# Pairing the head sums of queries and keys, and starting the last attention inside the projection before it

## The reference

```python
qkv_a, g_a, q_b, zf_fwd, zf_bwd, i_b, g_b, zgate_a, zgate_b = jnp.split(z, split_points, axis=-1)
qkv_a = qkv_a.reshape(B, S, N_GROUPS_2, 3, HEADS_PER_GROUP, HEAD_DIM)   # 3 groups, 8 heads, 64
for g, (window, dilation) in enumerate(ATTN_GROUPS):
    q = rms_norm(qkv_a[:, :, g, 0], q_norm_w[layer, g])
    k = rms_norm(qkv_a[:, :, g, 1], k_norm_w[layer, g])
    v = qkv_a[:, :, g, 2]
    o_g, m_g, d_g = dilated_window_attention(q, k, v, bias_tab[...], window, dilation)
...
o_a = jnp.sum(wts[..., None] * jnp.stack(outs), axis=0) / jnp.sum(wts, axis=0)[..., None]
y_a = (o_a * silu(g_a)) @ w_proj_a
...
y_b = (rms_norm(o_fwd + o_bwd, hg_norm_w) * silu(g_b)) @ w_proj_b
merged = sigmoid(zgate_a) * y_a + sigmoid(zgate_b) * y_b
h_res = h_res + merged @ w_out
```

## Time and profile before

| | us |
|---|---|
| median of 3 runs (lowest, highest) | 1845.63 (1845.46, 1846.04) |
| the profiled execution | 1845.46 |
| its span | 1843.7 |
| PE, PEld busy | 1722.3 (93%), 1435.8 (78%) |
| DVE, ACT busy | 1149.3 (62%), 1003.3 (54%) |
| POOL busy | 71.6 (4%) |
| mean granted clock of TensorE | 0.969 of full speed |

### The profile page before, as it was taken

How to read it: one execution, slowest core, us unless ns; L and a number is a source line. 1 busy time by engine, 2 the same in 40 slices (tenths; PEclk the granted TensorE clock), 3 DMA queues, 4 the chain that set the end, 5 groups by cost and what they waited for, 6 DMA issues and landing times.

```text
span 1843.7 us, 27871 instructions
## 1 busy us (share of the span) xinstructions
PE 1722.3 (93%) x11207; PEld 1435.8 (78%) x11212; DVE 1149.3 (62%) x1527; ACT 1003.3 (54%) x1314; POOL 71.6 (4%) x68
## 2 busy tenths in 40 slices
PE   6999989899999979999999699999979989999898
PEld 3786665698888748889869488888849978887588
DVE  5341664798989665333345698989855784534554
ACT  4323653488888644224343488888834562443452
POOL 0000000100000010000000000000010000100100
PEclk9999999899999979999999799999989999999999
DMA  8546004899999863223454499999944433353511
GB/s 332 193 122 228 1 15 196 326 400 406 408 404 407 333 282 120 101 100 137 182 215 186 160 364 408 406 407 405 378 171 180 180 144 139 86 212 137 146 61 69
DMA packets 53125, 421.76 MB, mean 229 GB/s; under 512 B 17044, under 2 KB 18196, under 8 KB 30624
## 3 DMA queue, kind: packets, MB, share of 16 engines
q1 hardware_dynamic: 26416, 364.55, 50.3%
q0 software_dynamic: 8592, 32.69, 5.6%
q10 hardware_dynamic: 18016, 23.07, 3.6%
HBM read 399.27 MB, written 21.02 MB: 228 GB/s over the span
## 4 chain that ended last, share of the span: by engine, by line
PE 82%; DVE 8%; ACT 4%; DMA 4%; issue 2%; POOL 1%; SPq 0%; ACTq 0%; DVEq 0%; POOLq 0%
PE ps L732 47%; PE ps L867 18%; PE ps L689 3%; DMA ring<-w_all 2%; PE ps L712 2%; PE ps L878 1%; PE ps L739 1%; DMA arena<-y_d,tok_row 1%; PE ps L723 1%; PE ps L1301 1%; PE ps L885 1%; PE ps L1103 1%; PE ps L1374 1%; PE ps L1132 1%; PE ps L1107 1%
## 5 line engine op out<-in xcount | busy, mean ns | idle before, releaser
L2211 DVE TENSOR_TENSOR w_lo<-ring,w_hi 128x1024 fp32r<-128x1024 f32 x384 | 452.5, 1219 | 55.4 <-ACT w_hi L1592 53.3
L1592 ACT ACTIVATE w_hi<-ring 128x1024 fp32r<-128x1024 f32 x384 | 396.3, 1057 | 97.3 <-PE ps L867 55.9
L732 PE MATMUL ps<-XT_lo,arena_r 128*128 128x256 f32 (+1 forms) x1712 | 386.5, 300 | 10.1 <-DVE ring_r L2081 7.2
L732 PEld LDWEIGHTS ps<-XT_lo,arena_r 128*128 128x128 f32 x1712 | 283.9, 190 | 25.9 <-issue 7.9
L867 PE MATMUL ps<-w_hi,x_hi 128*128 128x256 f32 (+1 forms) x768 | 248.5, 324 | 2.7 <-issue 2.6
L867 PE MATMUL ps<-w_lo,x_hi 128*128 128x256 f32 (+1 forms) x768 | 244.7, 319 | 0.0
L867 PE MATMUL ps<-w_hi,x_lo 128*128 128x256 f32 (+1 forms) x768 | 244.6, 319 | 0.0
L732 PE MATMUL ps<-arena_r 128*128 128x512 f32 (+1 forms) x656 | 233.1, 363 | 10.8 <-DVE XT_lo L2377 4.0
L2081 DVE TENSOR_TENSOR ring_r<-ring,arena_r 128x1024 fp32r<-128x1024 f32 x96 | 113.6, 1221 | 120.9 <-ACT arena_r L1494 120.8
L732 PE MATMUL ps<-XT_lo,ring_r 128*128 128x256 f32 x640 | 182.1, 285 | 0.0
L867 PEld LDWEIGHTS ps<-w_hi,x_hi 128*128 128x128 f32 x768 | 145.9, 190 | 19.4 <-DVE w_lo L2211 4.3
(11 more groups left out here) (350 smaller groups left out, 2690.3 us busy)
## 6 DMA issues: line engine op xcount, KB each, us to landing
ring<-w_all SPq DMA_DIRECT2D x172, 2048.0 KB, 9.5
y_d<-arena ACTq DMA_DIRECT2D x32, 512.0 KB, 10.0
arena<-toep_d POOLq DMA_DIRECT2D x16, 384.0 KB, 9.8
arena<-rpb ACTq DMA_DIRECT2D x16, 192.0 KB, 3.8
xtok_d<-arena ACTq DMA_DIRECT2D x6, 512.0 KB, 2.6
hT<-h SPq DMA_DIRECT2D x2, 1024.0 KB, 6.3
arena<-cb_d POOLq DMA_DIRECT2D x1, 1536.0 KB, 8.5
arena<-cc_d POOLq DMA_DIRECT2D x1, 959.0 KB, 5.6
```

The lines of the kernel that those rows point to most:

```text
L732: last = nc.tensor.matmul(out, a, b, start=(first and i == 0), stop=(final and i == 2))
L1592: nc.scalar.activation(w_hi[:, q], slot(b, "p (q c) -> p q c", q=4)[:, q], ACT.Copy).then_inc(hi_rdy, 1)
L2211: nc.vector.tensor_tensor(w_lo[:, q], slot(base + n, "p (q c) -> p q c", q=4)[:, q], as_f32(w_hi[:, q]), ALU.subtract).then_inc(*split_sig ...
```

## The change

Three things are edited, on three engines.

**Head sums in pairs of units.** `sum_heads(r)` now takes two units at once (`2r + 2` and `2r + 3`) with 4 matmuls. Each writes 32 rows, and the two units go to different groups of 32 partitions of bank 6: `r` even to rows 0 to 63, `r` odd to rows 64 to 127. It runs after the units 4, 6, 8, 10 and 12, and ahead of unit 14. The root and the reciprocal run over 128 rows instead of 48, and `spread_heads` reads 32 rows of them instead of 48.

**The first pair of the attention inside unit 19.** The units 18 and 19 accumulate in banks 4 and 5 (`z2_bank`) instead of 0 and 1. The scores of pair 0 (`at_scores(0)`) stand in unit 19 behind its first k, after a wait for `qn_done`. DVE makes pair 0 right behind its last scaling, and ACT its exponential ahead of copying out unit 19. The buffers of the probabilities (`probs2`) are laid out anew, so that the one of pair 0 doesn't overlap weights of unit 19.

**Fillers.** `last_split(0)` and `last_split(1)` go from ahead of the attention into its iterations 1 and 2 on ACT, and 2 and 3 on DVE. In iterations 8, 9 and 10 `gated_tile` stands ahead of the values and the turns.

```diff
-            def sum_heads(v):
-                pe.wait_ge(z2_ev, v + 3)
+            def sum_heads(r):
+                pe.wait_ge(z2_ev, 2 * r + 4)
                 for m in range(2):
-                    i = 2 * v + m
-                    last = nc.tensor.matmul(ps[0:48, 6, 0:SEQ], pick[:, 46 - 2 * i:94 - 2 * i], sq2[:, v % 2, m * SEQ:(m + 1) * SEQ],
-                                            start=(i == 0), stop=(i == 23))
+                    for b2 in range(2):
+                        j, at = 2 * (r % 2) + b2, 4 * (r // 2) + 2 * m
+                        last = nc.tensor.matmul(ps[32 * j:32 * j + 32, 6, 0:SEQ], pick[:, 46 - at:78 - at],
+                                                sq2[:, b2, m * SEQ:(m + 1) * SEQ], start=(at == 0), stop=(at == 10))
                 last.then_inc(qn_mm, 1)
...
-                        if u >= 3:
-                            sum_heads(u - 3)
+                        if u >= 4 and u % 2 == 0:
+                            sum_heads((u - 4) // 2)
...
+                            if u == 19 and k == 1:
+                                pe.wait_ge(qn_done, 12)
+                                at_scores(0)
+                            last = z_rows(56 + p, k, hf, ps[:, z2_bank(u), :])
...
-            pe.wait_ge(qn_done, 12)
-            pe.wait_ge(z2_ev, 20)
...
             for i in range(len(AT_PAIRS) + 3):
+                if 1 <= i < len(AT_PAIRS):
+                    at_scores(i)
+                if i == 2:
+                    pe.wait_ge(z2_ev, 20)
+                if i >= len(AT_PAIRS):
+                    gated_tile(i - len(AT_PAIRS))
                 if i >= 3:
...
-                if i >= len(AT_PAIRS):
-                    gated_tile(i - len(AT_PAIRS))
...
             for u in range(20):
+                if u == 19:
+                    at_exp(0)
                 act.wait_ge(z2_mm, u + 1)
...
                     if u >= 4:
-                        act.wait_ge(qn_mm, u - 3)
+                        act.wait_ge(qn_mm, (u - 4) // 2 + 1)
...
-            last_split(0)
-            last_split(1)
             for i in range(len(AT_PAIRS) + 2):
...
+                if 1 <= i < len(AT_PAIRS):
+                    at_exp(i)
+                if 1 <= i < 3:
+                    last_split(i - 1)
...
-            last_split(0)
-            last_split(1)
             for i in range(len(AT_PAIRS) + 3):
...
+                if 2 <= i < 4:
+                    last_split(i - 2)
```

More of the change, by code:

```diff
@@ L1370, in spread_heads, with at_scores @@
                     pe.wait_ge(qn_done, v)
+                rows = slice(32 * (v % 4), 32 * (v % 4) + 32)
                 for m in range(2):
-                    i = 2 * v + m
                     for e in range(2):
+                        i = rows.start + 4 * (v // 4) + 2 * m + e
                         last = nc.tensor.matmul(ps[half(e), 6, m * SEQ:(m + 1) * SEQ],
-                                                ident[0:48, 2 * i + e:2 * i + e + 1].broadcast_to([48, HD]), rr2,
-                                                start=True, stop=True)
+                                                ident[rows, i:i + 1].broadcast_to([32, HD]), rr2[rows], start=True, stop=True)
                 last.then_inc(qn_bc, 1)
+            def at_scores(i):
+                hp, q = AT_PAIRS[i]
+                if i:
+                    pe.wait_ge(sx_neg, AT0 + i)
+                for g in range(AT_G):
+                    for e in range(2):
+                        last = nc.tensor.matmul(ps[:, 2 * e + g // 2, (g % 2) * SEQ:(g % 2 + 1) * SEQ],
+                                                z2[half(e), 4 + 8 * g + hp, q * P:(q + 1) * P],
+                                                z2[half(e), 8 + 8 * g + hp, :], start=True, stop=True)
+                last.then_inc(sx_s, 1)
             for b in range(10):
@@ L1434, in _ @@
             for i in range(len(AT_PAIRS) + 3):
[L1435 to L1440, removed]
-                            last = nc.tensor.matmul(ps[:, 2 * e + g // 2, (g % 2) * SEQ:(g % 2 + 1) * SEQ],
-                                                    z2[half(e), 4 + 8 * g + hp, q * P:(q + 1) * P],
-                                                    z2[half(e), 8 + 8 * g + hp, :], start=True, stop=True)
-                    last.then_inc(sx_s, 1)
+                if 1 <= i < len(AT_PAIRS):
[4 more added lines that the diff above has]
+                    gated_tile(i - len(AT_PAIRS))
                 if i >= 3:
@@ L1950, in _, with at_exp @@
                 z_split(p)
+            def at_exp(i):
+                act.wait_ge(sx_neg, AT0 + i + 1)
+                for e in range(2):
+                    p2 = probs2[i % 3][e]
+                    last = nc.scalar.activation(p2, p2, ACT.Exp, scale=-1.0, bias=stat2[:, 8 * i + e:8 * i + e + 1],
+                                                accum_out=stat2[:, 8 * i + 2 + e:8 * i + 3 + e])
+                last.then_inc(sx_e, 1)
             for u in range(20):
+                if u == 19:
+                    at_exp(0)
                 act.wait_ge(z2_mm, u + 1)
-                src = ps[:, u % 6, :]
+                src = ps[:, z2_bank(u), :]
                 if u < 2:
@@ L1972, in _ @@
                 if u == 13:
-                    act.wait_ge(qn_mm, 12)
-                    nc.scalar.activation(rr2, ps[0:48, 6, 0:SEQ], ACT.Sqrt, bias=eps_col[0:48], scale=1.0 / HD).then_inc(qn_std, 1)
+                    act.wait_ge(qn_mm, 6)
+                    nc.scalar.activation(rr2, ps[:, 6, 0:SEQ], ACT.Sqrt, bias=eps_col, scale=1.0 / HD).then_inc(qn_std, 1)
             def last_split(p):
```

24 lines of the change are left out of this document (9 added, 15 removed).

## The result

The changed kernel takes **1835.47 us** (median of 5 runs, 1834.15 to 1836.96) against 1845.63 (5 runs, 1841.79 to 1846.10) of the kernel before: a ratio of 0.9944, 95% interval 0.9930 to 0.9957. The forecast was 1835.0, with a range from 1833.4 to 1838.2. The profiled execution took 1835.47 us with a span of 1833.7, 10.0 less than the span before.

The account below looks back on a forecast made before the run. PE, 82% of the chain, was taken to bound the kernel. Gains of 4.85 + 3.1 + 2.15 + 1.6 - 1.0 = 10.7 us took 1845.46 to 1834.8; 0.17 for the median gave 1835.0, range 1833.4 to 1838.2.

Parts of the forecast that it names:

- head sums: Projection: ten groups of 0.99 us leave the chain, five of 1.01 us come in, saving 4.85 us.
- first pair in unit 19: Between projection and attention: pair 0's scores inside unit 19 let the second scores begin 4.1 us earlier.
- splits as fillers: Attention's start: ACT's split ahead of the first copy of turned probabilities delays the first values, 1.0 us lost.
- the drain's wait filled, its fall gone, two new waits: Drain: `gated_tile(0)` fills a 2.15 us wait, the clock's fall goes (1.6 us won), new waits lose 1.0 us.
- a fall elsewhere: Rival: the clock falls behind the first values' longer wait, costing 1.6 us, for 1836.6 us; chance 0.18.
- The step from `spread_heads` to the new group: Projection: a new group of four matmuls was priced from the similar `spread_heads` row, 1.01 us.
- The late hand-over among the rivals: Rival: late scaling ahead of unit 19's scores, or the ring losing distance, costs some 2 us, for 1837; chance 0.11.
- the two new waits: Drain: PE waits 0.43 us for gating ahead of tile 3 and about 0.55 us at tile 4; 1.0 us lost.
- my own three signs of being wrong: Sums taking nearly 2 us a group, a clock fall in the loop's first rounds, tile 4 waiting over 1 us for DVE.
- the ring: Attention's loop, where PE, DVE and ACT wait on each other in turn; claimed to keep the 3.1 us gained.
- Half clock through the attention: Rival: the clock stays low from the first values, binding the loop by PE, 16.1 us more, 1851.1; chance 0.03.
- The row that I called sparse: Early in the kernel: a stretch with sparse matmuls at clock 0.50, cited for the half-clock rival.

Follow-up runs that it names:

- e1_sums: The kernel before with the change's paired head sums and nothing else; 1840.67 us against 1845.35, ratio 0.9974.
- e2_first_pair: The kernel before with the first pair inside unit 19 and the two splits as fillers, old head sums and drain order; 1843.47 us, ratio 0.9983.
- e3_drain: The kernel before with only `gated_tile` moved ahead of the values and turns in the drain; 1842.72 us, ratio 0.9983.
- e8_warm_both: The changed kernel with eight filler matmuls ahead of pair 2's scores and eight ahead of the first values' wait; 1832.05 us, ratio 0.9928.
- e7_drain_waits: e6 with the gating wait put behind tile 3's matmuls and DVE's `gated_out(0)` one split earlier; 1833.13 us, ratio 0.9926.
- after_again: The changed kernel run once more, unaltered, for a second trace; 1836.35 us (one run).
- e5: The changed kernel with eight filler matmuls ahead of the first values' wait; 1836.71 us (one run).
- e6: The changed kernel with ACT's second weight split one pair later and DVE's second split moved later too; 1834.43 us, ratio 0.9937.

## Why the prediction was right

The sum in the prediction came out at 10.7 us, and 10.0 of span and 10.2 of the median were measured. Term by term, from t0:

| term | predicted | measured | where |
|---|---|---|---|
| head sums | 4.85 | 5.01 | e1_sums, second scores |
| first pair in unit 19 | 4.1 | 4.06 | e2_first_pair, second scores |
| splits as fillers | -1.0 | -0.94 | e2_first_pair, fifth scores 3.12 |
| the drain's wait filled, its fall gone, two new waits | 2.15 + 1.6 - 1.0 = 2.75 | 3.23 | e3_drain, load |
| a fall elsewhere | 0 (rival) | -1.46 | e8_warm_both, fifth scores |

The measured terms add up to 9.9 us.

**Head sums.** The step from `spread_heads` to the new group held: 0.99 us against the 1.01 that I took. From the Trainium skill's figure for three column tiles (TensorE: Matmul & The Clock Gate, Measured speedup vs the span model) I had worked out 1.24 us a group as an estimate. That step from three tiles to two was mine, and it was too high: two column groups gave the full factor of two here. The measurement decides.

**The first pair.** The hand-overs were in time, as the timeline of DVE shows (L2770 the scaling, L2796 the reading of the scores):

```profile
1717.49 0.75 DVE L2770 SCALAR_TENSOR_TENSOR arena<-arena,sm,ps 128x512 f32<-128x512 f32 x1 [2.56 <-PE ps L1380]
1720.56 0.96 DVE L2796 CUSTOM_DVE_ANT_0 arena<-ps,arena 128x768 f32<-128x768 f32 x1 [2.32 <-PE ps L1391]
```

DVE's last scaling ends at 1718.24, and the scores in unit 19 begin at 1719.02. ACT ends the exponential at about 1724.4, and unit 19 ends at 1725.6. The late hand-over among the rivals didn't happen.

**The splits.** The first values wait 2.70 us, where I expected some 2.8.

**The drain.** The term that was mis-sized is that of the two new waits: 0.6 us (e7_drain_waits) instead of 1.0. The timeline of PE around tile 3 in the changed kernel:

```profile
1777.17 0.39 PE L736 MATMUL ps<-hT_r,arena_r 128*128 128x256 f32 x1 [0.39 <-DVE arena L2812]
...
1780.21 0.18 PE L698 MATMUL ps<-tick 128*32 128x2 bf16 x1
```

The wait ahead of tile 3 was as priced, 0.39 us idle against 0.43. That of tile 4 was not. The release before it ends at 1780.32 (1780.21 and 0.11) and tile 4 starts at 1780.45, 0.13 us instead of 0.55. DVE's queue took the 3.6 us that I counted (1776.83 to 1780.40), so the time that I gave tile 3 was too short: 1777.17 to the release at 1780.21 is 3.04 us, not 2.83. The sum was off as well: 3.6 less 0.3 + 2.83 + 0.11 is 0.36 us, and the 0.55 that I wrote has 0.19 that no row gives.

**The clock.** This is the step that failed by its likeliest case. I let the clock be 1.00 throughout, and gave 0.18 to a fall behind the first values' wait, at 1.6 us. That fall came, at the place named, and cost 1.46. A fall in the first rounds of the loop was one of my own three signs of being wrong, and it came. The forecast time was met to 0.5 us all the same, since the other terms were together 0.7 us better. That the two errors had opposite signs was luck. I argued against the fall from one wait of 3.44 us with none behind it. e1_sums shows a fall that begins as that very wait ends. One execution was no evidence that a wait is harmless, and a fall at the head of the ring deserved more than 0.18: six of the ten executions with at most one wait filled have one.

**Half clock through the attention** didn't happen in any of the six executions with a fall in the ring (e1_sums among them): each time full speed was back after 3.4 us. The row that I called sparse gave this rival no ground: PE is recorded busy for all of its 4.00 us. The rule of the Trainium skill on transposes (TensorE: Matmul & The Clock Gate, Part 4: PE-mode transpose) would keep the clock low in a ring one third of which is turns. The trace doesn't agree: the clock is 1.00 from 1744 to 1767.

## What to carry to other kernels

Matmuls with few output rows can go in pairs to different partition groups of one bank. Here that halved their cost, and a row of the same form elsewhere in the trace priced it to 0.02 us. Price a moved step by what stands ahead of it in each engine's queue: of the 0.95 us that a later place of ACT's split won at the first values, the ring gave back a third to a half. A wait on PE has two prices, its length and a fall of the clock behind it, and the second comes in some executions and not in others. So read it from several traces. A long wait is best filled with work that is due anyway, as `gated_tile` in the drain. Matmuls that nobody needs can fill it where they delay nothing; that this keeps the clock up is likely here, not proven.

## What the runs showed of the hardware that was not expected

**The clock's falls move between executions of one program.** Each fall lasted 3.4 us at 0.50, yet its cost wasn't the same: 1.46 us in the changed kernel, and 0.5 to 1.0 us where a wait followed that it could shorten (after_again, e5, e6, e7). One program had its fall at 1738.1 and at 1731.7, another in the tail or nowhere. The trunk ahead of the stage, the same in all kernels, varied from t0 = 1593.80 to 1600.09, and twelve runs of one kernel spread over 8.4 us (e1_sums, 1837.76 to 1846.15). For a gain of 3 us the place of a moment from a common start in two traces was the better measure; the medians needed twelve runs for it.

**A fall needs no long wait just ahead of it.** In after_again and e5_warm it follows a wait of 1.95 us between groups of 1.5 us, while the longer waits of 2.70 and 3.44 us are followed by none in e2_first_pair and in the kernel before. The three falls of the tail begin within 0.3 us of the end of a wait of 1.2 us, which follows shorter ones.
